# Two exact halves of an activation in one 512-column product, summed when the result leaves PSUM

## The reference

```python
for layer in range(2):
    x = x + (even_mixer if layer == 0 else odd_mixer)(rmsnorm(x, ...))   # mLSTM + pooling / gated linear attention
    x = x + peer_ffn(rmsnorm(x, f_norm[layer]), f_w_q[layer], f_sub_keys[layer], f_u[layer], f_v[layer])
return rmsnorm(x, final_norm)

def peer_ffn(...):                       # per token and head: 16 of 16384 experts
    q = xb @ w_q                         # 2048 x 2048
    s = q . keys                         # 8 heads x 2 x 128 key scores
    sv, si = top_k(s, 16)                # then the best 16 of the 16 x 16 sums
    a = xb . u[eid];  coef = softmax(cv) * gelu(a);  y = coef . v[eid]
```

## Time and profile before

| | us |
|---|---|
| median of three runs | 3901.87 (3900.09 to 3905.02) |
| the profiled execution | 3898.5 |
| its span in the trace | 3895.7 |
| PE busy | 3871.5 (99%) |
| DVE busy | 2516.7 (65%) |
| ACT busy | 2094.0 (54%) |

### The profile page before, as it was taken

One profiled execution on the slowest core, in us unless ns is written; L12 is line 12 of the kernel. 1 busy time (PEld: TensorE's weight loads), 2 busy tenths in 40 slices (PEclk: granted clock), 3 DMA queues, 4 the chain that ended last, 5 costly groups with the idle time before them and its releaser, 6 DMA issues.

```text
span 3895.7 us, 72477 instructions
## 1 busy us (share of the span) xinstructions
PE 3871.5 (99%) x25484; PEld 3556.0 (91%) x25484; DVE 2516.7 (65%) x3845; ACT 2094.0 (54%) x3368; POOL 170.8 (4%) x148
## 2 busy tenths in 40 slices
PE   9999999999999999999999999999999999999999
PEld 8989999999998888888899889999999998888887
DVE  4565688778886555555565555778788875555555
ACT  5354444478885444444454544444688874444444
POOL 2110000010000000000121000000100000000000
PEclk9999999999999999999999999999999999999999
DMA  5445555555545566655454455555555455666665
GB/s 201 146 168 179 181 181 182 183 173 169 171 169 185 195 197 198 197 194 195 164 176 145 168 176 188 182 183 183 178 168 172 168 176 193 197 200 201 200 196 182
DMA packets 194870, 706.80 MB, mean 181 GB/s; under 512 B 22256, under 2 KB 22448, under 8 KB 194400
## 3 DMA queue, kind: packets, MB, share of 16 engines
q1 hardware_dynamic: 190800, 692.21, 53.7%
q0 software_dynamic: 3984, 13.37, 0.9%
HBM read 699.20 MB, written 6.29 MB: 181 GB/s over the span
## 4 chain that ended last, share of the span: by engine, by line
PE 98%; DVE 1%; DMA 1%; ACT 1%; issue 0%; DVEq 0%; SPq 0%; ACTq 0%
PE ps L1658 17%; PE ps L1659 17%; PE ps L1660 17%; PE ps L2042 12%; PE ps L2044 12%; PE ps L2043 12%; PE ps L2026 2%; PE ps L1741 1%; PE ps L1743 1%; PE ps L1742 1%; PE ps L1950 1%; PE ps L1949 1%; PE ps L1951 1%; PE ps L1726 1%; PE ps L1880 0%; DVE act_lo_t L1125 0%
## 5 line engine op out<-in xcount | busy, mean ns | idle before, releaser
L1066 DVE TENSOR_TENSOR w_lo<-w_raw,w_hi 128x1024 fp32r<-128x1024 f32 x1312 | 1628.1, 1243 | 1261.1 <-ACT w_hi L565 1245.9
L565 ACT ACTIVATE w_hi<-w_raw 128x1024 fp32r<-128x1024 f32 x1312 | 1389.6, 1060 | 1333.0 <-DMA w_raw<-in_v_tab 759.6
L1658 PE MATMUL ps<-act_lo_t,w_hi 128*128 128x256 f32 x5504 | 1562.9, 284 | 4.3 <-DVE act_lo_t L1125 3.1
L1659 PE MATMUL ps<-act_hi_t,w_lo 128*128 128x256 f32 x5504 | 1557.9, 283 | 0.0
L1660 PE MATMUL ps<-act_hi_t,w_hi 128*128 128x256 f32 x5504 | 1556.5, 283 | 0.0
L1658 PEld LDWEIGHTS ps<-act_lo_t,w_hi 128*128 128x128 f32 x5504 | 1053.8, 191 | 8.2 <-issue 6.3
L1660 PEld LDWEIGHTS ps<-act_hi_t,w_hi 128*128 128x128 f32 x5504 | 1055.4, 192 | 0.0
L1659 PEld LDWEIGHTS ps<-act_hi_t,w_lo 128*128 128x128 f32 x5504 | 1054.9, 192 | 0.1
L2042 PE MATMUL ps<-w_hi,act_lo_t 128*128 128x512 f32 x2048 | 797.8, 390 | 0.1
L2043 PE MATMUL ps<-w_lo,act_hi_t 128*128 128x512 f32 x2048 | 796.9, 389 | 0.0
L2044 PE MATMUL ps<-w_hi,act_hi_t 128*128 128x512 f32 x2048 | 796.9, 389 | 0.0
(11 more groups left out here) (242 smaller groups left out, 2211.7 us busy)
## 6 DMA issues: line engine op xcount, KB each, us to landing
w_raw<-in_u SPq DMA_DIRECT2D x512, 512.0 KB, 3.2
w_raw<-in_v_tab SPq DMA_DIRECT2D x512, 512.0 KB, 3.7
w_raw<-in_dense SPq DMA_DIRECT2D x288, 512.0 KB, 3.3
x_spill<-big POOLq DMA_DIRECT2D x16, 256.0 KB, 4.4
big<-x_spill POOLq DMA_DIRECT2D x32, 128.0 KB, 4.0
big<-in_x_in SPq DMA_DIRECT2D x4, 512.0 KB, 4.7
big<-in_keys POOLq DMA_DIRECT2D x2, 1024.0 KB, 7.6
out<-big SPq DMA_DIRECT2D x8, 256.0 KB, 2.1
```

Of the source, the lines that this page charges most:

```text
L565: act.activation(w_hi[:, slot, :], w_raw[:, slot, :], ACT.Copy).then_inc(s_hi, 1)
L1066: dve.tensor_tensor(w_lo[:, slot, :], w_raw[:, slot, :], w_hi[:, slot, :].bitcast(F32), ALU.subtract).then_inc(s_lo, 1)
L1658: pe.matmul(out, wh, xl, start=start, stop=False, **kw)
L1659: pe.matmul(out, wl, xh, start=False, stop=False, **kw)
```

## The change

The halves of an activation now lie side by side (`act_t`), so that one product of 512 columns with w_hi serves both; the product of w_lo with act_hi adds to the first 256 columns. A block then stands in PSUM as two parts of 256 columns, a main part (hi x hi + lo x hi) and a second part (hi x lo), which are added as the block leaves: ACT copies one part aside, DVE adds the other (`join`). In `u` the sum goes back to PSUM and ACT's Gelu reads it there; in `o` ACT's sigmoid follows in place. The 64 blocks of each layer beside which PE scatters keep the old form (`wide=False`).

```diff
-        act_hi_t = sb("act_hi_t", [P, KB, T], F32R)
-        act_lo_t = sb("act_lo_t", [P, KB, T], F32R)
+        act_t = sb("act_t", [P, KB, 2, T], F32R)
+        act_hi_t, act_lo_t = act_t[:, :, 0, :], act_t[:, :, 1, :]
...
PE:
+            def two_wide(b, wh, wl, kb):
+
+                pe.matmul(bank(b), wh, act_t[:, kb, :, :], start=kb == 0, stop=False)
+                return pe.matmul(bank(b, T), wl, act_hi_t[:, kb, :], start=False, stop=kb == KB - 1)
...
+                    if wide:
+                        ins = two_wide(b, w_hi[:, slot, c], w_lo[:, slot, c], kb)
+                        continue
                     ins = three(ps[:, b, 0:T], w_hi[:, slot, c], w_lo[:, slot, c], act_hi_t[:, kb, :],
...
ACT, blocks to SBUF (qk, p, o, r; q_evac likewise):
-                    act.activation(dst, bank(par, T), func, scale=scale).then_inc(s_evac, 1)
+                    act.activation(dst, bank(par, T), ACT.Copy).then_inc(s_aside, 1)
...
ACT, phase o:
+                def sigmoid(b):
+                    act.wait_ge(s_joined, b + 1)
+                    act.activation(at(E_SO + T * b, T), at(E_SO + T * b, T), ACT.Sigmoid).then_inc(s_evac, 1)
...
ACT, phase u:
+                def aside(b, par):
                     act.wait_ge(s_used, b * 2 + (ubase + 2))
-                    dst = at(b * T, T) if isinstance(b, int) else big[:, bass.ds(b * T, T)]
-                    act.activation(dst, bank(par, T), ACT.Gelu).then_inc(s_evac, 1)
+                    act.activation(direct(b), ps[:, par, T:2 * T], ACT.Copy).then_inc(s_aside, 1)
+
+                def joined(b):
+                    act.wait_ge(s_joined, b + (M_BLOCKS + DIRECT * layer + 1))
+
+                def gelu(b, par):
+                    act.activation(direct(b), bank(par, T), ACT.Gelu).then_inc(s_evac, 1)
...
                 def u_turn(i):
                     for s in range(8):
+                        if s % 2 == 0:
+                            joined(i * 4 + (s // 2 - 2))
                         hi(s % 4, i * 8 + (ubase + s))
                         if s % 2:
-                            ge(i * 4 + (s // 2 - 1), (s // 2 + 1) % 2)
+                            aside(i * 4 + (s // 2 - 1), 1 - s // 2 % 2)
+                        else:
+                            gelu(i * 4 + (s // 2 - 2), s // 2 % 2)
...
                 c_hi(1, 1)
-                root_table()
                 hi(2, vbase + 2)
...
                 v_blocks(0, range(2, V_TURN))
+                root_table()
...
DVE:
+            def join(name, layer, b, par):
+                dve.wait_ge(s_aside, b + (BLOCK0[name, layer] + 1))
...
+                if name == "u":
+
+                    dve.tensor_tensor(bank(par, T), bank(par, T), dst, ALU.add).then_inc(s_joined, 1)
+                else:
+                    dve.tensor_tensor(dst, dst, ps[:, par, T:2 * T],
+                                      ALU.add).then_inc(s_joined if name == "o" else s_evac, 1)
...
-                def topk_turn(item, n0, slabs):
+                def topk_turn(item, n0, slabs, name, first):
...
                     for s in slabs:
                         lo(s % 4, n0 + s)
                         for _ in range(per):
                             if steps:
                                 steps.pop(0)()
+                        if s % 2:
+                            join(name, layer, first + s // 2, 1 - s // 2 % 2)
...
                 with dve.Fori(1, ITEMS - 1) as i:
-                    topk_turn(i + 1, i * 8 + ubase, range(8))
+                    topk_turn(i + 1, i * 8 + ubase, range(8), "u", i * 4 - 1)
...
-                chain(dve.tensor_copy(rstd[:, :], bank(4, T)))
-                chain(dve.tensor_copy(jw[:, 0, :], rstd[:, :]))
-                chain(dve.tensor_tensor(jw[:, 1, :], rstd[:, :], jw[:, 0, :].bitcast(F32), ALU.subtract))
+                chain(dve.tensor_copy(jw[:, 0, :], bank(4, T)))
+                chain(dve.tensor_tensor(jw[:, 1, :], bank(4, T), jw[:, 0, :].bitcast(F32), ALU.subtract))
```

More of the change, by code:

```diff
@@ L606, in stream, with block_to @@
                 pending[0] = last
-            def block_to(name, layer, o, func=ACT.Copy, width=T, skip=0, scale=1.0, hi_part=None):
+            def block_to(name, layer, o, width=T, skip=0):
                 n0 = SLAB0[name, layer]
@@ L774, in even @@
                     evac(b)
-                    next_two("o", 0, b)
+                    n = SLAB0["o", 0] + 2 * b + 4
+                    hi(n % RING, n)
+                    sigmoid(b)
+                    hi((n + 1) % RING, n + 1)
                     if b in beside:
@@ L781, in even @@
                 hi(0, n)
+                sigmoid(6)
                 act.wait_ge(s_pool_out, 8)
@@ L788, in even @@
                 evac(7)
+                sigmoid(7)
                 for h in range(M_HEADS):
@@ L909, in q_evac @@
                         act.wait_ge(s_sc_ps, b + 16 * layer)
-                    act.activation(at(K_QS + T * par, T), bank(par, T), ACT.Copy).then_inc(s_evac, 1)
+                    act.activation(at(K_QS + T * par, T), bank(par, T), ACT.Copy).then_inc(s_aside, 1)
                 s_turn = [0]
@@ L988, in mix_turn @@
                         weighted(i, s)
+                        if isinstance(i, int) and i == SC_FIRST and s == 0:
+                            joined(DIRECT - 2)
+                            gelu(DIRECT - 2, 0)
+                        if isinstance(i, int) and i == SC_FIRST and s == 2:
+                            joined(DIRECT - 1)
+                            gelu(DIRECT - 1, 1)
                         if s % 2:
@@ L991, in mix_turn @@
                             if isinstance(b, int) and b < DIRECT:
-                                ge(b, b % 2)
+                                aside(b, b % 2)
                             else:
@@ L1077, in stream @@
                         lo(s, i * RING + (n0 + s))
+                        if s % 2:
+                            join(name, layer, i * 2 + (s // 2 - 1), 1 - s // 2)
             def v_groups(layer, ngroups):
@@ L1160, in even @@
                 stream("qk", 0, 16)
-                ahead(SLAB0["v", 0])
+                ahead(SLAB0["v", 0], ("qk", 0, 7))
                 rows = lambda r: big[0:4, E_ROWS + T * r:E_ROWS + T * (r + 1)]
@@ L1231, in even @@
                 for b in range(8):
+                    join("p", 0, b, b % 2)
                     if b == 6:
@@ L1243, in even @@
                 for b in range(6):
+                    join("o", 0, b, b % 2)
                     next_two("o", 0, b)
@@ L1249, in even @@
                 n = SLAB0["out", 0]
+                join("o", 0, 6, 0)
                 lo(0, n)
@@ L1254, in even @@
                 gated(2)
+                join("o", 0, 7, 1)
                 gated(3)
@@ L1330, in odd @@
                 for b in range(KB):
+                    join("qk", 1, b, b % 2)
                     next_two("qk", 1, b)
@@ L1337, in odd @@
                     n = SLAB0["r", 1] + 2 * b + 4
+                    join("r", 1, b, b % 2)
                     lo(n % RING, n)
@@ L1475, in experts @@
                 lo(1, ubase + 8 * (SC_FIRST - 1) + 1)
+                join("u", layer, DIRECT - 5, 1)
                 dve.wait_ge(s_cexp, layer + 1)
@@ L1537, in scatter_turn @@
                         lo(s % 4, i * 8 + (ubase + 8 * SC_FIRST + s))
+                        if isinstance(i, int) and i == 0 and s == 1:
+                            join("u", layer, DIRECT - 1, 1)
                         if s % 2 == 0 and pair:
@@ L1549, in experts @@
                     lo(s % 4, ubase + 8 * (SC_FIRST - 1) + s)
+                join("u", layer, DIRECT - 2, 0)
                 scatter_turn(0)
```

46 lines of the change are left out of this document (34 added, 12 removed).

## The result

| | before | after |
|---|---|---|
| median of four runs, us | 3900.98 (3899.57 to 3905.02) | 4006.63 (4005.63 to 4007.61) |
| ratio, 95% interval | | 1.0269 [1.0251, 1.0287] |
| the profiled execution, its span, us | 3898.5, 3895.7 | 4007.61, 4005.9 |
| a turn of `u` with the search, us | 23.04 | 26.84 |
| the same at PE's pace for 64 steps, us | 23.04 | 22.2 or 22.6 (below) |

The account below looks back on a forecast made before the run. PE's issue time bounds the kernel now; in `u`'s search turns DVE and ACT would. 3898.5 - 46.3 + 116.6 + 4 = 3972.8 us for the profiled execution, the median 3.4 above: 3976 us, range 3945 to 4010.

Parts of the forecast that it names:

- The bound and the mechanism: In `u`'s search turns: DVE and ACT, waiting on each other, become the bound instead of PE; 26.4 us against 22.14.
- The cycle join, `hi`, `lo`: In `u_turn`: ACT waits for DVE's join before even slabs' `hi`, DVE's `lo` waits for that `hi`; turn 26.4 us.
- DVE's own work: In a search turn of `u`: DVE's time from each `lo` until it could start the next, 20.02 us in sum.
- The four detours: Four times a turn of `u`: join, handover to ACT, `hi`, handover back before `lo`; 1.60 us each.
- Handovers are dearer: Rival, search turns of `u`: handovers of 0.2 us each, detour 1.87, turn 27.5, 30 us more, 4005; chance 0.12.
- PE's gain: All 3456 changed steps: 359.4 ns becomes 346.0, 46.3 us off if PE stays the bound throughout.
- 13.4 ns go with each product: PE's products of 256 and 512 columns: 13.4 ns of each product's time doesn't depend on its columns.
- The merged product saves nothing: Rival, PE's merged steps: cost goes with columns, PE's turn stays 23.0 us, 3998 us in all; chance 0.05.
- The other phases: Outside `u`'s search turns: joins in `p` and `o` and the sigmoid's hop add 4 us, between 0 and 10.
- 116.6: Turns 1 to 14 of `u`: time lost to the lengthened loop, 58.3 us a layer, 116.6 us in both.
- The clock: Rival, PE's new gaps in `u`'s turns: clock falls to 1.2 GHz, at most 78 us more, 4054; chance 0.03.

Follow-up runs that it names:

- e1: Changed kernel with ACT's wait for the join moved behind `hi`, plus a one-column copy: 3881.39 us, 0.9962 of the kernel before.
- e2: Changed kernel with the join right behind the odd slab's `lo`, ahead of its search steps: 3884.19 us, 0.9969 of the kernel before.
- e7: Changed kernel with ACT's wait moved behind `hi` at slabs 2 and 6 of each turn only: 3935.97 us, 1.0102 of the kernel before.
- e10: Changed kernel with the two products of a step swapped in every second step: 3997.57 us, 1.0257 of the kernel before.
- e4: Kernel before with the merged product alone, no join or copy aside, w_hi x act_lo left out: 3869.18 us, 0.9928 of the kernel before.
- e3: Changed kernel with `u` back in its old form, other phases as changed: 3896.91 us, 1.0001 of the kernel before.
- e8: e1 with the sigmoid of block 0 in `o` moved behind the sums of squares: 3878.18 us, 0.9954 of the kernel before.

## Why the prediction was right, and where it missed

**The bound and the mechanism: right.** The cycle join, `hi`, `lo` is in the rows as described, and e1, e2, e7 and e10 each show it from another side.

**DVE's own work: 20.02 forecast, 20.41 measured.** From the rows above, 2.67 + 2.81 + 2.80 + 3.32 + 2.39 + 3.85 + 1.43 + 1.14. The three joins that stand behind a search step start 0.24 to 0.26 us after it ends, where I had put the 0.12 of a `lo`: they wait for the step itself.

**The four detours: 4 x 1.60 = 6.40 forecast, 6.43 measured** (1.56 + 1.65 + 1.56 + 1.66). Turn 26.84 instead of 26.4. Over 13 turns in two layers that is 11.4 us. "Handovers are dearer" fell: the detour is 1.61, not 1.87. That its 4005 us is so close to the measured 4006.6 is chance.

**PE's gain: the term that was mis-sized most.** "13.4 ns go with each product" gave 46.3 us. e4 gives 28. The separate streams of 256 and 512 columns each have one pace; the mixture has two. I had bounded the saving by 0 and 13.4 and taken the upper end, "because it is what those two sizes show". They don't show a mixture. "The merged product saves nothing" was too hard as well. The rule of the Trainium skill (TensorE: Matmul & The Clock Gate, "Back-to-back issue gap"), N/2.4 + 2.5 ns, which the page calls the gap of isolated products, would have saved 2.5 ns a step; neither pace agrees with it.

**The other phases: +4 forecast, about +10 measured**, the upper end. e3 has 10 us more of PE's waits than before. Its 1408 merged steps outside the turns should have given 9.4 (at 6.7 ns) to 18.9 us, and the total is 0.

**The sum.** Forecast for the stretches of `u` with the search: 116.6 less the gain of 2048 steps there, 27.4, is +89.2; measured +104.2, of which 11.4 is the longer turn. For all others: 4 less 18.9 is -14.9; measured +6.0. Of these 20.9 up to 9.4 are the slower pace and 6 the waits beyond the 4. The rest, 5.5 us or more, may be the clock: outside the turns it fell six times in the version after (at 196, 251, 2104, 2114, 2138 and 2148 us) and three times in the kernel before, and one fall costs up to 1.7 us (below), so three more cost up to 5; no run tests that. The two make 36 us between forecast and measured growth of the span, and 31 between 3976 and the median. Both errors have the same sign; the range held because it took in the dearer detour and the useless merge, neither of which came true. So the sign and the turn were worked out rightly, and that 4006.6 lies inside 3945 to 4010, 3.4 us from its end, is in part luck.

**The clock: it did fall, and in the turns it cost nothing.** This was a rival with a chance of 0.03, for a fall that shows in the time. In the version after, around the wait for slab 4 of a turn, columns as in the earlier trace rows:

```profile
632.00:634.00 2.00, 2.00 (x13) 1.62 (x11) 1.26 (x4) 0.34 (x1) 0.00 (x0) 1.00 0.72 178
634.00:636.00 2.00, 0.17 (x2) 0.00 (x0) 1.25 (x3) 2.00 (x4) 0.00 (x0) 1.00 0.58 125
636.00:638.00 2.00, 1.97 (x7) 1.69 (x8) 1.77 (x5) 0.21 (x1) 0.00 (x0) 0.57 0.56 221
638.00:640.00 2.00, 2.00 (x8) 1.68 (x8) 1.84 (x4) 0.00 (x0) 0.00 (x0) 0.57 0.00 0
```

After a standstill of 1.85 us the next 4 us have a granted clock of 0.57, most of it at the lower level of 1.2 GHz, and 7 to 8 products in 2 us in place of 13. Six steps take 3.75 us where 2.1 is usual, 1.7 us more. There are 19 such falls in the 28 turns. The turn shown above, from 593.09 us, has standstills of 1.82 and 1.98 us and no fall, and at 26.84 us it is as long as those with one. The prediction had PE wait in front of slabs 2, 4 and 6, some 115 us in all. The waits are mostly before slabs 4 and 6:

```profile
609.18 0.50 PE L1738 MATMUL ps<-act_t,w_hi 128*128 128x512 f32 x1 [1.82 <-DVE w_lo L1101]
616.98 0.50 PE L1738 MATMUL ps<-act_t,w_hi 128*128 128x512 f32 x1 [1.98 <-DVE w_lo L1101]
```

Of PE's 101 us of waits some 76 belong to the turns (101 less the 24.6 of e3), 2.7 us each; the other part of its 4.2 us of air it spent on slower products. The turn's length is DVE's sum all the same, since PE is ready again in time.

**Not settled.** What puts the mixed stream into its fast or slow state; and what the rest of the 10 us of new waits in the other phases is, beside the 3.1 us piece behind POOL and the 2.6 us of the sigmoid. One microsecond of it isn't the joins': PE waits 9.1 us for the first normalisation in e4 too, which has none, after 8.1 before.

## What to carry to other kernels

When an edit adds a wait, write down what is queued behind the waiting instruction, and ask whether the engine it waits for needs any of that next. If it does, the two engines form a cycle whose length is a sum of durations, and it can be the bound though neither is full: DVE was busy for 76% of the stretch in `u` and ACT for 39%. Here the remedy was order: nearly the same instructions with the wait behind `hi` went from 2.7% slower to 0.4% faster. The paces of two uniform streams didn't give that of their mixture here: the saving taken from them, 13.4 ns, was reached in some stretches and halved in others.

## What the runs showed of the hardware that was not expected

At a granted clock of 1.00 a stream of load and product, alternating 512 and 256 columns, runs at 346.6 or 353.3 ns for the pair. In e4 it stays there for hundreds of microseconds; in e8 it changes several times within `u`. 512, 256, 256, 512 runs at 348.3, and 256 first at 352.8. The difference of 6.7 ns is 23 us over the kernel's 3456 steps, half of what the merge can gain. And `lo`, 1.23 us on an undisturbed DVE, took 4.79 and 2.93 us beside subtractions on POOL, each time until 1.1 us after POOL's instruction; when `lo` started first, by 0.17 us, it was POOL's instruction that took longer, 4.75 us instead of 3.85.
